# The last row tile's first half: scaled by ScalarE and stored by an adding transfer, in place of finished by VectorE and stored plainly

## The reference

```python
y = merged @ w_out[l]
h = layer_norm(alpha * h + y, ln_g[l], ln_b[l])

def layer_norm(x, g, b):
    mu = jnp.mean(xf, axis=-1, keepdims=True)
    var = jnp.mean(jnp.square(xf - mu), axis=-1, keepdims=True)
    y = (xf - mu) * lax.rsqrt(var + LN_EPS)
    return y * g + b
```

## Time and profile before

| | |
|---|---|
| median of three executions | 1801.15 us |
| the profiled execution | 1802.3 us, its span 1800.5 us |
| mean granted TensorE clock | 0.997 |
| TensorE busy | 1785.9 us, 99% |
| VectorE / ScalarE / GpSimd busy | 77% / 51% / 14% |
| HBM read and written | 314.84 MB and 105.50 MB |

### The profile page before, as it was taken

The page is one execution under the profiler, slowest core; times in us unless marked ns, Lnnn a source line. Parts: engine busy times, 40 slices in busy tenths (PEclk is TensorE's granted clock), DMA queues, the critical chain, the costliest instruction groups (busy, mean ns, idle before and its releaser), DMA issues.

```text
span 1800.5 us, 24208 instructions
## 1 busy us (share of the span) xinstructions
PE 1785.9 (99%) x8341; PEld 1483.9 (82%) x8341; DVE 1381.4 (77%) x2248; ACT 918.8 (51%) x1552; POOL 247.9 (14%) x315
## 2 busy tenths in 40 slices
PE   9999999999999999999999999999999999999997
PEld 7888888888888888888888888888888888888886
DVE  5777774887777787577778878788789788967778
ACT  5663332555464646444445455455555666745543
POOL 1111111100222221011100101101111100003123
PEclk9999999999999999999999999999999999999998
DMA  9585776960866554597877958768596978959989
GB/s 335 182 212 161 195 204 197 270 234 5 237 179 177 162 147 142 175 244 180 211 211 189 268 107 245 190 172 246 117 283 144 302 259 287 296 173 245 238 210 193
DMA packets 258825, 370.18 MB, mean 206 GB/s; under 512 B 15089, under 2 KB 142129, under 8 KB 255409
## 3 DMA queue, kind: packets, MB, share of 16 engines
q1 hardware_dynamic: 185712, 215.25, 37.3%
q0 software_dynamic: 72880, 153.55, 36.6%
q10 hardware_dynamic: 144, 0.26, 0.0%
HBM read 314.84 MB, written 105.50 MB: 233 GB/s over the span
## 4 chain that ended last, share of the span: by engine, by line
PE 98%; DVE 1%; DMA 0%; issue 0%; ACT 0%; POOL 0%; POOLq 0%; DVEq 0%; SPq 0%; ACTq 0%
PE acc L813 10%; PE acc L815 10%; PE acc L814 10%; PE scores L1025 6%; PE scores L1027 6%; PE scores L1029 6%; PE acc L1025 3%; PE acc L1027 3%; PE acc L1029 3%; PE transposed L838 3%; PE attended L1027 2%; PE attended L1029 2%; PE attended L1025 2%; PE scores L1255 2%; PE scores L1259 2%; PE scores L1257 2%
## 5 line engine op out<-in xcount | busy, mean ns | idle before, releaser
L1507 ACT ACTIVATE piece_split<-w 128x512 fp32r<-128x512 f32 x448 | 282.5, 632 | 290.4 <-PE scores L1029 104.8
L2161 DVE TENSOR_TENSOR piece_split<-w,piece_split 128x512 fp32r<-128x512 f32 x448 | 308.5, 690 | 104.9 <-ACT piece_split L1507 94.6
L2013 DVE TENSOR_TENSOR w_lo<-raw_weights,w_hi 128x1024 fp32r<-128x1024 f32 x211 | 256.4, 1219 | 123.5 <-ACT w_hi L1402 121.7
L813 PE MATMUL acc<-h_hi,w_lo 128*128 128x512 f32 x800 | 319.2, 399 | 0.0
L815 PE MATMUL acc<-h_hi,w_hi 128*128 128x512 f32 x800 | 312.6, 391 | 0.0
L814 PE MATMUL acc<-h_lo,w_hi 128*128 128x512 f32 x800 | 311.8, 390 | 0.0
L1402 ACT ACTIVATE w_hi<-raw_weights 128x1024 fp32r<-128x1024 f32 x211 | 223.1, 1060 | 108.9 <-PE acc L815 27.4
L815 PEld LDWEIGHTS acc<-h_hi,w_hi 128*128 128x128 f32 x800 | 150.2, 188 | 32.2
L813 PEld LDWEIGHTS acc<-h_hi,w_lo 128*128 128x128 f32 x800 | 150.4, 188 | 30.0 <-issue 1.8
L814 PEld LDWEIGHTS acc<-h_lo,w_hi 128*128 128x128 f32 x800 | 150.6, 188 | 28.6
L1025 PE MATMUL scores<-piece_split,h_lo 128*128 128x512 f32 x384 | 149.8, 390 | 0.0
(11 more groups left out here) (541 smaller groups left out, 3694.2 us busy)
## 6 DMA issues: line engine op xcount, KB each, us to landing
w<-in_w_in SPq DMA_DIRECT2D x128, 512.0 KB, 9.3
raw_weights<-in_w_in SPq DMA_DIRECT2D x102, 512.0 KB, 5.0
anch_weight_sums_scratch<-in_w_branch POOLq DMA_DIRECT2D x30, 1024.0 KB, 10.2
raw_weights<-anch_weight_sums_scratch SPq DMA_DIRECT2D x40, 512.0 KB, 5.6
raw_weights<-in_w_branch SPq DMA_DIRECT2D x38, 512.0 KB, 5.8
raw_weights<-in_w_mem_kv SPq DMA_DIRECT2D x32, 512.0 KB, 5.5
gate_scratch<-in_b_gate POOLq DMA_DIRECT2D x12, 1024.0 KB, 12.0
anch_weight_sums_scratch<-anch_weight_sums_scratch POOLq DMA_DIRECT2D x10, 1024.0 KB, 8.1
```

Source lines behind the costliest of these rows:

```text
L813: pe.matmul(bank_out, wl, hi[:, k, :], start=first, stop=False)
L1507: act.activation(p_split[:, n % RING, 0, :], sources[p][:, k, :], ACT.Copy).then_inc(pc_hi, 1)
L2013: dve.tensor_tensor(w_lo[:, slot, :], raw[:, slot, :], w_hi[:, slot, :].bitcast(F32), ALU.subtract).then_inc(lo_ready, 1)
L2161: dve.tensor_tensor(p_split[:, n % RING, 1, :], sources[p][:, k, :], p_split[:, n % RING, 0, :].bitcast(F32), ALU.subtract).then_inc(pc_lo, 1)
```

## The change

The first half of the last tile (columns 0 to 1023 of tile 3) takes the adding form. VectorE now centres its three parts one after the other and finishes only the second and the third. ScalarE scales the first half (`scale`, with the sixth count of `centred`) ahead of its own plain store. GpSimd issues a sixth adding store behind it. SyncE's plain store of that half is gone, and the closing waits count one plain store fewer and one adding store more.

```diff
-OUT_STEPS = 12 + 4 * TT + 12
+OUT_STEPS = 12 + 4 * TT + 12 - 1
@@ SyncE
             sp.dma_start(out_t[TT - 2][:, BW:D], resid[:, TT - 2, BW:D]).then_inc(parts_stored, 16)
-            sp.wait_ge(last_part, 2)
-            sp.dma_start(out_t[TT - 1][:, 0:BW], resid[:, TT - 1, 0:BW]).then_inc(parts_stored, 16)
-            sp.wait_ge(last_part, 4)
+            sp.wait_ge(last_part, 3)
             sp.dma_start(out_t[TT - 1][:, BW + 512:D], resid[:, TT - 1, BW + 512:D]).then_inc(parts_stored, 16)
-            sp.wait_ge(parts_stored, 64)
-            sp.wait_ge(out_stored, 16 * (2 * (TT - 1) - 1))
+            sp.wait_ge(parts_stored, 48)
+            sp.wait_ge(out_stored, 16 * 2 * (TT - 1))
@@ ScalarE
             act.activation(small[:, 2, TT - 1:TT], mv[:, TT - 1, 1:2], ACT.Copy, bias=LN_EPS).then_inc(eps_added, 1)
-            act.wait_ge(last_part, 3)
+            scale(TT - 1, slice(0, BW), 6)
+            act.wait_ge(last_part, 2)
             act.dma_start(out_t[TT - 1][:, BW:BW + 512], resid[:, TT - 1, BW:BW + 512]).then_inc(parts_stored, 16)
@@ VectorE
-            steps.mark(centre(3, first))
+            centre(3, first).then_inc(centred, 1)
             steps.mark(centre(3, second))
+            steps.mark(centre(3, third))
             steps.settle()
             dve.wait_ge(rstd_ready, TT + 4)
             dve.wait_ge(b2_loaded, 16)
-            finish(3, first)
-            steps.mark(centre(3, third))
             finish(3, second)
-            steps.settle()
             finish(3, third)
@@ GpSimd
             rstd(3)
+            store_tile(3, slice(0, BW), 6)
```

## The result

The changed kernel takes 1805.6 us (1805.0 to 1806.36, 11 runs), the kernel before beside it 1801.2 us (1800.75 to 1802.13, 11 runs): a ratio of 1.0023, 95% interval [1.0014, 1.0031], +4.4 us. The forecast was 1802.2 with a range to 1804.6. The loss is clear of noise and outside the range.

A forecast was written before the change was run, and what follows sets the result against it. TensorE bounds the kernel, and only the tail of some 11.5 us can move: VectorE's 1.2 us are given back and 1.0 more by the new store's later landing, taking the median from 1801.15 to 1802.2 us, range 1800.2 to 1804.6.

The forecast's parts named there:

- What bounds the kernel: Whole run: TensorE is busy 99% of 1800.5 us; only the tail of some 11.5 us can move.
- VectorE, ScalarE, the issues: Tail: VectorE done 1.2 us earlier, ScalarE's ACTIVATE hidden, GpSimd's new issue at 1794.25, SyncE's last store leaving at 1795.12.
- The landing, 1801.1: End of the tail: the new adding store lands last, 6.9 us behind its issue, instead of 1800.1: +1.0 us.
- the slow start: GpSimd's new adding store: its delay is mostly hidden by work ahead; 0.7 us left for it and the receipt.
- something common to both releases it (my forecast, no cost): Closing barrier: GpSimd's drain, ending at 1800.2, is released together with SyncE's last steps, at no cost.
- my second rival: Closing barrier: GpSimd's drain ends 2.4 us behind its own last store's landing; +3.3 us, 1804.45, chance 0.10.
- the drain from the issue: Closing barrier, rival: GpSimd's drain ends 10.5 us behind its last store's start; +4.5 us, 1805.65, chance 0.06.
- differences are carried over to the median as they are: Whole kernel: differences in the profiled execution, 1802.3 us and 1.15 us above the median of 1801.15, apply to the median.
- The rule on late engines: DMA tail: by a Trainium skill rule, GpSimd's new store adds to the late engine's delay, nearer 8.1 than 5.6 us.
- the 5.6 row: Profile row for adding stores: landing 5.6 us behind issue in a free queue, which would put the new one at 1799.85.
- the 8.1 row: Profile row for adding stores: tile 2's half landed 8.1 us behind issue, which would put the new one at 1802.35.

The follow-up runs named there:

- e7: Changed kernel with tile 2's first half centred, scaled and stored first: 1805.41 us, ratio 1.0022 to the kernel before.
- e8: Changed kernel with tile 2's first half stored plainly on ScalarE's queue, its offset left out: 1805.43 us, ratio 1.0022 to the kernel before.
- e4: Changed kernel with GpSimd's sixth store plain on the same queue, that half's offset left out: 1802.59 us, ratio 1.0007 to the kernel before.
- e3: Kernel before plus a 16 KB plain GpSimd store, issued when VectorE has finished the last tile's first half: 1802.3 us, ratio 1.0006.
- e5: Kernel before plus a 16 KB plain GpSimd store, issued only when VectorE has finished the last part: 1803.75 us, ratio 1.0013.
- v5: Kernel before, tile 2's first half centred first; last tile's first 512 columns scaled by ScalarE, offset added on GpSimd, stored plainly: 1802.03 us, ratio 1.0003.
- v1: Kernel before with VectorE centring tile 2's first half ahead of its second, nothing left out: 1801.23 us, ratio 0.9998.
- e6: Kernel before with tile 2's first half stored plainly on ScalarE's queue, its offset left out: 1800.91 us, ratio 0.9996.
- e2: Changed kernel with the first halves of tile 2 and the last tile stored plainly on ScalarE's queue, offsets left out: 1800.54 us, ratio 0.9993.
- e1: Changed kernel with the last tile's first half stored plainly on ScalarE's queue, its offset left out: 1801.66 us, ratio 0.9999 to the kernel before.

## Why the prediction was wrong, point by point

**What bounds the kernel** was right in place: only the tail moved.

**VectorE, ScalarE, the issues**: right to a tenth. VectorE's end 1795.24 with a last matmul 0.14 us later (forecast 1795.10), the ACTIVATE at 1792.92 (1792.82), the sixth issue at 1794.37 (1794.25), SyncE's last at 1795.27 (1795.12).

**The landing, 1801.1**: the number was met, 1801.10, but by luck. I had built it as tile 2's half ahead in the queue plus 2.6 us of packets, with the slow start mostly hidden by the work ahead and 0.7 us for it and the receipt. e7 and e8 took that half forward or away and the landing stayed: the work ahead cost nothing, and the slow start was paid in full. The times of single packets in e8 give the sum: 1.9 us from the issue to the first packet (1.8 in e7 and the changed kernel), 0.5 to 2.1 us for the first packet on each engine, 2.3 for the other seven at 0.33, 0.8 for SyncE's eight packets of 0.10 that take turns with them, 0.4 from the last packet to the landing. That is an estimate of 5.9 to 7.5 us for the 7.1 measured. The first packets are also what the stretch 1796 to 1797 above shows (DMA busy 1.52 at only 172 GB/s). In e4 the plain packets took 0.17 us, the first ones too. Why the start and the first adding packets are so slow is open. SyncE's last part was forecast to land at 1798.9 and landed at 1801.3; that it would take turns with the adding store I had not seen, but it ends before the drain and costs nothing here.

**The step that failed** is "something common to both releases it (my forecast, no cost)": I took GpSimd's drain in the kernel before, level with SyncE's last steps to a tenth, for one that ends with them. It was level by chance: one engine brought tile 2's half in at 1797.80, 1.8 us behind the other fifteen (1795.99), and SyncE's last part was late too. What the runs show in its place, an end 2.45 us behind the landing of GpSimd's last store, was my second rival, at 0.10. What GpSimd does in these 2.45 us no run shows. That rule turns a landing at 1801.1 into an end at 1803.8, which is the span. The rival whose number fits best, the drain from the issue with 1805.65, is wrong as a mechanism (e3, e5): its 4.5 us agree with the measured 4.4 by accident.

**Why 4.4 and not 3.3**: "differences are carried over to the median as they are" failed too. The profiled run of before (1802.3) is 1.1 us above its median because one DMA engine was late. In 33 runs beside e5 to v5 the kernel before gave 20 times 1800.55 to 1801.40 and 13 times 1801.81 to 1802.92. The traces of e3, e5 and v1, whose last plain part is that of before, show what I take for an ordinary end: that part lands at 1799.10, 1799.36 and 1799.09, not 1800.08. From there the change costs 2.0 us of landing (1799.1 to 1801.1) and 2.3 more of drain (2.47 behind the landing, where SyncE's own closing step took 0.2): 4.3 us. In the profiles of the changed kernel, e7 and e8 it is the drain that ends the kernel.

**The rule on late engines.** It did not come into play: the sixth store's engines landed within 1.1 us of each other (1800.04 to 1801.10), 6.7 us behind the issue and nearer to the 5.6 row than to the 8.1 row. e6, with no adding store in the last 7 us, has no engine at work behind the others: from 1798.4 to 1799.0, DMA busy 0.00, and its runs spread over 0.7 us where those of before spread over 2.4.

```profile
1798.40:1799.00 0.60, 0.00 (x0) 0.00 (x0) 0.00 (x0) 0.00 (x0) 0.00 (x0) 0.50 0.00 0
```

The Trainium skill, as the prediction named it ("DMA: Bandwidth & Descriptors", "Latency and other measured facts"), calls two engines usually slower and gives GpSimd's transfers as a guess at the cause. e6 and e2 agree, but v1 and e3 have an adding store and no engine over a microsecond late at the last landing, so it is a risk here, not a fixed price. In both profiles with a late engine (before and e1) one packet of tile 2's adding store took 2.57 and 2.58 us, where none of that store took over 1.43 in the others; that fits as the cause, but no run tests it.

## What to carry to other kernels

A store issued by GpSimd is not paid when it lands: in this kernel GpSimd's closing drain adds 2.45 us behind it, and even 16 KB at the end cost 2.5 us, so it is worth trying the last stores of a kernel on the other queues. When an instruction of the closing barrier ends level with another engine's last step, compute when it would end by a rule of its own before you take it for hidden. Do not count on work ahead in a queue to hide a store's slow start: e8 tells the two apart. And check that the one profiled run is an ordinary one before a difference from it is carried to the median: here it was 1.1 us late.

## What was not expected of the hardware

- GpSimd's DRAIN ended 2.42 to 2.47 us behind its last store's landing in nine kernels, and 3.5 to 3.6 us behind its last instruction in the three where the stores had landed by about then; the drains of ScalarE take 0.15 us with a store in flight.
- The adding store of 512 KB at the end landed 6.7 to 7.1 us behind its issue whether its queue was empty or not, with no packet in the first 1.8 to 1.9 us where the queue was empty and first packets of up to 2.1 us; a plain one on the same queue took 4.3 us; and a plain store of 256 KB on SyncE's queue beside the adding one took 6.0 to 6.4 us in place of 2.5 to 3.8 (5.3 behind a late engine).
- A GpSimd addition of 128x512 made a VectorE instruction of two SBUF inputs last 1.77 us instead of 0.74 (v5). The Trainium skill, "SBUF — State Buffer", section "Who interferes with whom", says that a VectorE instruction with two SBUF inputs and a GpSimd instruction that reads SBUF contend; the trace agrees, with 1.03 us.
